# Two attentions, a latent part and a mixer's end reordered in a 2-block fp32 transformer kernel

## The reference

```
o = from_blocks(lax.map(block_fn, ...))            # A: softmax over picked keys, B: stick-breaking
return (o * jax.nn.silu(gate)) @ w_o
...
mod = cond @ w_mod + b_mod                         # cond = silu(c); six rows of 2048
h = _rmsnorm(x, pre_mix_g) * (1.0 + scale_a) + shift_a
proj = h @ w_in                                    # q_lat, kv_lat, k_rope, hq, f_fwd, f_bwd, hi, hg
attn_out = _mla(...)                               # rmsnorm(q_lat) @ w_uq, rmsnorm(kv_lat) @ w_ukv, rope, softmax
rec_out = _hgrn2_bidir(...)
mix = jnp.concatenate([attn_out, rec_out], axis=-1) @ w_out
x = x + gate_a * _rmsnorm(mix, post_mix_g)
h = _rmsnorm(x, pre_mlp_g) * (1.0 + scale_m) + shift_m
y = jnp.square(jax.nn.relu(h @ w_up)) @ w_down     # 2048 -> 8192 -> 2048
x = x + gate_m * _rmsnorm(y, post_mlp_g)
```

## Time and profile before

| | us |
|---|---|
| median of 3 runs | 2210.45 (2209.52 to 2211.97) |
| the profiled execution | 2210.13 |
| its span | 2208.3 |
| TensorE busy | 2170.7 |
| VectorE busy | 1429.2 |
| ScalarE busy | 1028.2 |

### The profile page before, as it was taken

How to read it: one execution, slowest core, us unless ns; L and a number is a source line. 1 busy time by engine, 2 the same in 40 slices (tenths; PEclk the granted TensorE clock), 3 DMA queues, 4 the chain that set the end, 5 groups by cost and what they waited for, 6 DMA issues and landing times.

```text
span 2208.3 us, 24626 instructions
## 1 busy us (share of the span) xinstructions
PE 2170.7 (98%) x10387; PEld 1808.1 (82%) x10387; DVE 1429.2 (65%) x1408; ACT 1028.2 (47%) x1044; POOL 7.2 (0%) x17
## 2 busy tenths in 40 slices
PE   8999999999999999999999999999999999999998
PEld 8878888877888788778788988877888888888887
DVE  5778667775756777877966676486445545544646
ACT  5443563433436643444454566575433433443442
POOL 0000000000000000000100000000000000000000
PEclk9999999999999999999999999999999999999999
DMA  8867649575976557758952325355556655655753
GB/s 289 311 243 271 248 153 364 205 292 183 366 270 231 189 223 296 274 193 355 346 178 98 129 86 200 115 229 215 204 193 230 225 191 210 248 191 191 267 182 123
DMA packets 73070, 497.25 MB, mean 225 GB/s; under 512 B 9040, under 2 KB 9472, under 8 KB 16384
## 3 DMA queue, kind: packets, MB, share of 16 engines
q1 hardware_dynamic: 72640, 495.59, 61.6%
q10 hardware_dynamic: 320, 0.09, 0.0%
HBM read 491.42 MB, written 4.23 MB: 224 GB/s over the span
## 4 chain that ended last, share of the span: by engine, by line
PE 91%; DVE 5%; ACT 2%; DMA 2%; issue 1%; DVEq 0%; SPq 0%; ACTq 0%
PE products L2395 65%; PE products L2406 14%; PE aside L2714 1%; DMA raw<-in_w_c_f 1%; PE transposed L2833 1%; DVE w_low L1470 1%; PE transposed L2471 1%; ACT w_high L851 1%; DVE raw L1484 1%; PE transposed L2561 1%; PE aside L2561 1%; PE transposed L2529 1%; DVE w_low_spare L1470 0%; PE products L2820 0%; PE aside L2820 0%
## 5 line engine op out<-in xcount | busy, mean ns | idle before, releaser
L1470 DVE TENSOR_TENSOR w_low<-raw,w_high 128x2048 fp32r<-128x2048 f32 (+3 forms) x323 | 714.4, 2215 | 551.6 <-ACT w_high L851 550.9
L851 ACT ACTIVATE w_high<-raw 128x2048 fp32r<-128x2048 f32 (+3 forms) x323 | 597.7, 1853 | 802.1 <-PE products L2395 635.9
L2395 PE MATMUL products<-w_high,x_high 128*128 128x512 f32 (+2 forms) x1664 | 641.7, 386 | 13.6 <-DVE w_low L1470 10.9
L2395 PE MATMUL products<-w_high,x_low 128*128 128x512 f32 (+2 forms) x1664 | 634.1, 381 | 0.0
L2395 PE MATMUL products<-w_low,x_high 128*128 128x512 f32 (+2 forms) x1664 | 633.9, 381 | 0.0
L2395 PEld LDWEIGHTS products<-w_high,x_high 128*128 128x128 f32 x1664 | 313.3, 188 | 73.7 <-issue 13.2
L2395 PEld LDWEIGHTS products<-w_high,x_low 128*128 128x128 f32 x1664 | 313.2, 188 | 59.2
L2395 PEld LDWEIGHTS products<-w_low,x_high 128*128 128x128 f32 x1664 | 313.3, 188 | 58.5 <-issue 1.7
L1484 DVE SCALAR_TENSOR_TENSOR raw<-raw,cond_row 128x2048 f32<-128x2048 f32 x96 | 220.3, 2295 | 0.8 <-DMA raw<-in_w_mod 0.8
L2395 PE MATMUL products<-w_high,u_high 128*128 128x512 f32 x496 | 193.7, 391 | 0.0
L2395 PE MATMUL products<-w_high,u_low 128*128 128x512 f32 x496 | 193.0, 389 | 0.0
(11 more groups left out here) (442 smaller groups left out, 2113.3 us busy)
## 6 DMA issues: line engine op xcount, KB each, us to landing
raw<-in_w_mlp SPq DMA_DIRECT2D x128, 1024.0 KB, 4.9
raw<-in_w_mod SPq DMA_DIRECT2D x96, 1024.0 KB, 5.1
raw<-in_w_ple SPq DMA_DIRECT2D x32, 1024.0 KB, 6.6
raw<-in_w_a_qkv SPq DMA_DIRECT2D x24, 1024.0 KB, 5.8
raw<-in_w_b_kvq SPq DMA_DIRECT2D x24, 1024.0 KB, 6.9
raw<-in_w_a_gate SPq DMA_DIRECT2D x16, 1024.0 KB, 6.1
raw<-in_w_a_out SPq DMA_DIRECT2D x16, 1024.0 KB, 7.2
raw<-in_w_b_gate SPq DMA_DIRECT2D x16, 1024.0 KB, 6.1
```

What stands on the lines that cost most here:

```text
L851: act.activation(split_tile(m, 0, st, u, j, 0, n), m.raw[:, RAW_SLOT[at], 0:n], ACT.Copy).then_inc(m.s_w_high, 1)
L1470: dve.tensor_tensor(lo, m.raw[:, RAW_SLOT[at], 0:n], hi.bitcast(F32), ALU.subtract).then_inc(m.s_raw_used, 1)
L2395: ins = pe.matmul(bank, x[:, x0 + kk, a], w, start=first and kk == 0 and n == 0, stop=last and kk == st.kq - 1 and n == 2)
```

## The change

Four places are written in another order. (a) Attention A: the four key heads of both row blocks are roped first, with half of the memset as the signal, the query heads behind. (b) Attention B: the last b_gate product is stored by a plain copy between the logarithms of groups 2 and 3, and its Silu is taken later, behind x_high of group 1; the gating of group 2 stands ahead of x_low of group 1. (c) Block C's latent part: two of three pieces of proj_mla are turned ahead of the last heads_slot; the last head's finish, low of ukv and c_oh, and ScalarE's copies of mla_kv are reordered. (d) The mixer's end: unit 0 of c_om is multiplied for row block 1 only up to j = 1; j = 2 and 3 of row block 1 stand behind all of row block 0. The mlp's units 0 and 1 are multiplied together: row block 0 with all eight quarters, then row block 1. All eight split quarters are kept in slots until then; one of the new spare slots is the memory of `cond_row`, so the cond row is loaded again behind them, its Silu taken in the mlp, and the mod tiles start two units later. The normed columns and thrown squares go into the PSUM banks `aside`.

```
-    ("c_om", 2, (0, 0), 4, 512), ("mlp", 32, (0, 2, 2, 0, 0, 0, 0, 0) * 4, 4, 512),
+    ("c_om", 2, (0, 0), 4, 512), ("mlp", 32, (0, 0, 0, 2, 2, 0, 0, 0) + (0, 2, 2, 0, 0, 0, 0, 0) * 3, 4, 512),
...
-SPARE_SLOTS = ((18432, 20480), (13312, 15360), (8192, 6144), (8192, 14336), (12288, 16384))
+SPARE_SLOTS = ((18432, 20480), (13312, 15360), (8192, 6144), (12288, 16384), (8192, 14336), (None, 22528), (10240, 4096))
...
-    m.h_cols = at("mlp_normed_columns", 22528, [P, 2, 512])
-    m.mix_sq = at("mix_squares", 23552, [P, 2, 512])
+    m.h_cols = m.u
...
-TURNS_MLP = {0: [(0, 2)], 1: [(0, 3)], 3: [(0, 4), (2, 5)], 4: [(0, 6)], 5: [(0, 7)]}
+TURNS_MLP = {(0, 0, 0): [(2, 3)], (1, 0, 2): [(3, 4)], (1, 0, 3): [(1, 5)], (0, 1, 0): [(1, 6)], (0, 1, 1): [(1, 7)]}
...
+    def cond_again():
+
+        sp.wait_ge(m.s_w_used, 4 * (PLAN["mlp"].g0 + 1) + 4 + 2)
+        bring(m.cond[:], rows(d.c, D), m.s_cond_landed)
...
-        load_unit("mlp", u, {(0, 1): x_rows})
+        load_unit("mlp", u, {(0, 0): x_rows, (2, 3): cond_again})
...
-    gemm("b_gate", keep(m.pb, 3072, ACT.Silu), late=2, aside=softplus_aside)
-    logs((2, 3))
+    def gate_kept(st, i, k):
+        if (i, k) == (1, 1):
+            logs([2])
+            keep(m.pb, 3072)(st, i, k)
+            logs([3])
+        else:
+            keep(m.pb, 3072, ACT.Silu)(st, i, k)
+
+    gemm("b_gate", gate_kept, late=2, aside=softplus_aside)
...
     group_high(1, m.s_b_ogt, m.s_b_xh)
+    act.wait_ge(m.s_g_free[1], (gate.s0 + gate.units) // 2 + 1)
+    last_gates = m.pb[:, :, 3072 + 1536:3072 + 2048]
+    act.activation(last_gates, last_gates, ACT.Silu).then_inc(m.s_b_gate3, 1)
...
+        if n == 6 * HH - 1:
+            latent_high(0)
+            latent_high(1)
         heads_slot(n)
...
-        if j < 3:
-            high_unit("c_oh", 0, [j])
-        if j == 1:
+        if j == 0:
             head_columns(14, 1)
+            high_unit("c_oh", 0, [0])
+        if j >= 2:
+            high_unit("c_oh", 0, [j - 1])
...
-    for rb in range(RB):
-        rope(m.pa[:, rb, 0:(NH + NKV) * HD].rearrange("p (h e) -> p h e", e=HD)[:, :, 0:2 * ROT_A], NH + NKV, ROT_A, 0, rb, m.a_rope)
-    dve.memset(m.a_nm[:], 0.0).then_inc(m.s_a_roped, 1)
+    for n, (first, heads) in enumerate(((NH, NKV), (0, NH))):
+        for rb in range(RB):
+            rope(m.pa[:, rb, HD * first:HD * (first + heads)].rearrange("p (h e) -> p h e", e=HD)[:, :, 0:2 * ROT_A], heads, ROT_A, 0, rb, m.a_rope)
+        dve.memset(m.a_nm[:, 2 * n:2 * n + 2], 0.0).then_inc(m.s_a_roped, 1)
...
     low_unit("b_out", 0, [2])
+    gate_group(2)
     group_low(1, m.s_b_xh, m.s_b_done)
-    gate_group(2)
...
-        for rb in range(RB):
-            ins = half(om, 0, j, m.g[:, 2 * k + rb], rb, 0, True, True)
+        for rb in range(RB if j < 2 else 1):
+            ins = half(om, 0, j, m.g[:, 2 * k + rb], rb, 0, True, j < 2)
...
+    for j in range(4):
+        pe.wait_ge(m.s_raw_used, quarter_at(om, 1, j) + 5)
+        half(om, 1, j, m.g[:, MIX_BANKS[0][j]], 0, 4, j < 2, True).then_inc(m.s_om_rows, 1)
+    for j in (2, 3):
+        pe.wait_ge(m.s_mix_added, j - 1)
+        half(om, 0, j, m.g[:, MIX_BANKS[1][j]], 1, 0, True, False).then_inc(m.s_w_used, 1)
+    early = {2: {0: lambda: turn(0), 2: lambda: turn(1)}, 3: {2: lambda: turn(2)}}
+    for j in range(4):
+        if j < 2:
+            pe.wait_ge(m.s_mix_added, 3 + j)
+        half(om, 1, j, m.g[:, MIX_BANKS[1][j]], 1, 4, j < 2, True, early.get(j)).then_inc(m.s_w_used, 1)
...
+    def first(st):
+        for rb in range(RB):
+            for u in range(2):
+                for c in range(4):
+                    between = {at: (lambda nth=nth: turn(nth)) for at, nth in TURNS_MLP.get((u, rb, c), ())}
+                    ins = half(st, u, c, m.g[:, 2 * u + rb], rb, 4 * c, c == 0, c == 3, between)
...
-    add_row(7, 0)
     mix_gain(0, 2)
+    first(0)
+    mix_gain(0, 3)
+    inverse_std(0, 1)
     dve.wait_ge(m.s_res2_landed, 16)
...
+    low_unit("mlp", 1, [1])
+    added(1, 3)
+    low_unit("mlp", 1, [2])
     second(1)
+    inverse_std(1, 2)
     scaled(1, 0)
+    low_unit("mlp", 1, [3])
```

More of the change, by code:

```diff
@@ L78 @@
 BY_ROWS = ("c_hi", "c_mla", "c_hg")
-PRODUCTS = {"uq": 4, "ukv": 4, "c_oh": 4, "c_om": 8}
+PRODUCTS = {"uq": 4, "ukv": 4, "c_oh": 4, "c_om": 6}
 LEAD = {0: (0, 0, 0, 0, 0), 2: (0, 0, 1, 1, 2), 3: (0, 0, 1, 2, 3)}
@@ L341, in memory @@
     m.hi, m.lo = sb("w_high", [P, RING, 2048], F32R), sb("w_low", [P, RING, 2048], F32R)
-    m.spare = [[at(f"w_{part}_spare_{n}", word, [P, 2048], F32R) for part, word in zip(("high", "low"), words)] for n, words in enumerate(SPARE_SLOTS)]
     m.xh, m.xl = sb("x_high", [P, KT, T], F32R), sb("x_low", [P, KT, T], F32R)
@@ L348, in memory @@
     m.cond = sb("cond_row", [P, D])
+    m.spare = [[nc.alloc_sbuf_tensor_at(f"w_{part}_spare_{n}", [P, 2048], F32R, offset=nc.lookup_mloc(m.cond).addr) if word is None
+                else at(f"w_{part}_spare_{n}", word, [P, 2048], F32R) for part, word in zip(("high", "low"), words)] for n, words in enumerate(SPARE_SLOTS)]
     m.modc = sb("mod_columns", [P, MOD_TILES])
@@ L552, in memory @@
     m.s_b_done = sem("b_done")
+    m.s_b_gate3 = sem("b_last_gate")
     m.s_m_ready = sem("m_ready")
@@ L1440, in quarter @@
                 mlp_high(q, 5, [1, 2])
-            elif k < 7 or not last:
+            elif (q, k) == (0, 0):
+                mlp_high(0, 2, range(3))
+            elif (q, k) != (0, 1) and (k < 7 or not last):
                 mlp_high(q, k + 1, range(3))
@@ L1448, in quarter @@
                 u_high(q, k - 1)
-            if k < 7 or not last:
+            if (q, k) > (0, 0) and (k < 7 or not last):
                 mlp_high(q, k + 1, [3])
+            if (q, k) == (0, 1):
+                act.wait_ge(m.s_cond_landed, 32)
+                act.activation(m.cond[:], m.cond[:], ACT.Silu).then_inc(m.s_cond_ready, 1)
     for q in range(4):
@@ L2153, in vector_program @@
         if rb == 0:
+            low(ukv, 0, [3])
             head_columns(14, 1)
@@ L2331, in hidden_quarter @@
                 low(mlp, 8 * q + 5, [1, 2])
-            elif k < 7 or not last:
+            elif (q, k) == (0, 0):
+                low(mlp, 2, range(3))
+            elif (q, k) != (0, 1) and (k < 7 or not last):
                 low(mlp, 8 * q + k + 1, range(3))
@@ L3058, in hidden_quarter @@
                 first(mlp)
+            elif first and k == 1:
+                pass
             elif k == 4:
```

219 lines of the change are left out of this document (123 added, 96 removed).

## The result

The changed kernel takes 2193.03 us (median of 4 runs, 2193.0 to 2195.17); the kernel before, timed beside it, 2210.12 (4 runs, 2209.52 to 2211.97). The ratio is 0.9924, with a 95% interval of 0.9909 to 0.9939: 17.1 us, 0.8%, faster. The forecast was 2193.8 (2191.0 to 2199.5). The profiled execution took 2193.03 too, its span is 2191.2 against 2208.3.

What follows compares the result with a forecast made beforehand. TensorE, busy 98% of the span, bounds the kernel, so only its waits and slow clock can go. 0.9 + 2.3 + 3.75 + 9.1 = 16.05, with 0.55 start-up 16.6 us off: about 2193.8 us, range 2191.0 to 2199.5.

Steps and rivals of the forecast that it cites:

- Attention A, 0.9: Attention A: roping key heads first makes keys ready near 215, removing TensorE's a_neg_max wait; 0.9 us, bounds 0 to 0.9.
- Attention B, 2.3: Attention B: earlier logarithms remove the 1.49 us b_scores wait, earlier group 2 gating b_out_gated's 0.82; bounds 1.5 to 2.5.
- Latent part, 3.75: Block C: waits for x_low (1.80), proj_hq (1.01) and mla_kv (1.04) go, less 0.1 new wait; bounds 2.0 to 4.0.
- Mixer's end, 9.1: Mixer's end into mlp: put-off quarters and joint units cover both row blocks' chains; gain 9.1 us, bounds 4.5 to 10.
- The late column of row block 0: Mixer's end: the last column of row block 0 was counted 0.4 us late, leaving that much wait.
- The first rival: Mixer's end: tight places with about half a us to spare are late, 3 to 5 us come back, 2197 to 2199; chance 0.20.
- the fourth: Rival: a new wait inside the mixer slows the clock again, losing 5 to 7 us, 2199 to 2201; chance 0.06.
- The slow clock: Behind the mixer's-end wait, TensorE's reduced clock cost 1.2 us in one stretch and some 0.6 in the next.
- The columns in PSUM, 0: Normed columns and thrown squares written to PSUM: the SBUF time of 1.49 us for four kept, no gain in the sum.
- Cond row, 0: Mlp: reloading the cond row and taking its Silu later costs 0, with 10 us to spare.
- The third rival: Loads queued behind the cond row's come late, making the whole slower, 2215 for 0.2%; chance 0.03.
- start-up: Slower first matmuls behind each removed wait, up to 0.2 us each; 0.55 us together for the earlier parts.

Runs made afterwards that it cites:

- all three undone: Changed kernel with attention A's key-heads-first rope, attention B's reordered logarithms and its early gating of group 2 all undone: 2197.94 us.
- the two runs show: Changed kernel with block C's whole latent part undone: 2196.46 us; with only its latent columns put behind the last heads_slot again: 2196.00 us.

## Why the prediction was right

**Attention A, 0.9.** Right, 1.12 with the slower matmuls behind the wait. In the timeline after, the keys' rope starts at 213.35 and the signal's memset stands at 215.23, where the prediction had about 215:

```profile
213.35 0.49 DVE L1604 TENSOR_TENSOR a_rope<-proj_a,cos_sin 128x128 f32<-128x128 f32 x2
...
215.23 0.07 DVE L1745 MEMSET a_neg_max<- 128x16 f32 x1
```

That it shows in the time is not shown by its own run (+0.2), only by the traces and by the run with all three undone.

**Attention B, 2.3.** Right, 2.72. ScalarE after, in the order of the earlier trace rows:

```profile
754.67 1.02 ACT L918 ACTIVATE proj_b<-products 128x1024 f32<-128x1024 f32 x1 [0.57 <-PE products L2450]
...
757.18 1.28 ACT L1139 ACT_TABLE_LOAD   x1
```

The product's copy now waits 0.57 us, for 2.16 in the earlier trace rows, and the table of Exp is loaded at 757.18 where the forecast said 757.6. The Silu put off ends at 781.7 and group 3's gating, at 784.05 on VectorE, waits for none of it. Undone singly, the logarithms cost 1.7; the gating brought its 0.82 us wait back and, by the rows, 1.0 to 1.1 us, but only 0.2 in the median.

**Latent part, 3.75.** Right, 3.91. The new wait is 0.3 us for mla_kv ahead of ukv's last product; 0.1 for w_low was expected. The wait for x_low goes for another reason than the other two, as the two runs show; those two were not undone singly.

**Mixer's end, 9.1.** Right, 9.57, and by its own steps. ScalarE, VectorE and TensorE there after:

```profile
1460.31 0.49 DVE L2295 TENSOR_SCALAR mix<-residual,rstd 128x512 f32<-128x512 f32 x1
...
1462.04 0.60 PE L3112 MATMUL transposed<-const,mix 128*128 128x128 f32 x4
...
1465.33 1.47 ACT L1402 ACTIVATE aside<-transposed,mlp_norm_columns 128x128 f32<-128x128 f32 x4
...
1485.61 0.49 DVE L2295 TENSOR_SCALAR mix<-residual,rstd 128x512 f32<-128x512 f32 x1
...
1488.30 0.60 PE L3112 MATMUL transposed<-const,mix 128*128 128x128 f32 x4
```

The first turn's rows are ready at 1460.8 and used at 1462.04: 1.2 us to spare, forecast 1.0. Row block 1's first rows are ready at 1486.1 and used at 1488.3: 2.2 to spare, forecast 1.9. The late column of row block 0 costs 0.19 us, forecast 0.4. Between c_oh and unit 2 the waits went from 7.1 us to 0.2 and TensorE's busy time fell by 2.6, where the forecast had 7.1 to 0.4 and 2.4 (1.8 of clock and 0.6 of small change). The first rival, that these slacks would go, didn't come, nor did the fourth, a new wait in the mixer; in the ten profiles that have the new order whole, the wait at that column is 0.49 at most. That TensorE's cover decides, and not the work moved, is shown by the two runs that change its order alone: they lose 3.44 and 7.29 us at the very turns where cover was taken away, 4.1 and 8 expected.

**The slow clock.** It was counted with 1.8 us, and TensorE's clock now reads 1.00 all through the mixer's end. By the granted clocks of the earlier trace rows it cost some 5 x 0.11 + 5 x 0.23 = 1.7 us, an estimate; the other 0.9 of the 2.6 us of busy time are then the slower matmuls behind the four waits. The Trainium skill (TensorE: Matmul & The Clock Gate, Part 1: The HAM clock gate) has an idle array fall back to the halved rate; the runs agree, the stretches with or behind waits of 3.44, 4.41 and 7.29 us read 0.77, 0.50 and 0.50.

**The columns in PSUM, 0.** Four scalings take 1.46 to 1.48 us after and took 1.49 to 1.51 before (the earlier trace rows has one). The tip of the Trainium skill (ScalarE: Activation LUTs, Step-by-step: what each stage is for), that PSUM is the faster destination for ScalarE, agrees in its direction; it is worth some 0.03 us per column here.

**Cond row, 0.** Right: 9.4 us to spare for the Silu. The third rival, the slower side, was about the loads behind the cond row's; the two waits for w_low in the list after stand at the start (8.9) and at c_f's end (1.46), none in the mlp, so those loads were not late either.

**What was mis-sized** is little. The earlier three parts gave 7.75 for 6.95, so 0.80 beyond their waits where 0.55 was allowed for start-up, and the mixer's end gave 0.47 more than its 9.1: 0.7 too little in all. The loss of 0.76 at the start and the gain of 0.58 at c_f's end, which nobody forecast, nearly cancel each other. So the profiled execution gained 17.1 us for 16.6 forecast; that it came so near is owed to mechanisms and sizes that were right, and in part to luck, since such events alone move other profiled runs by 2 to 5 us.

**What stays open.** Why the wait at c_f's end varies was not tried. Whether the 0.58 us there belong to the change can't be said: in eight profiles whose programs are the same up to that place it is between 0.88 and 2.80 us. Whether the loads there set its length is not shown either.

## What to carry to other kernels

Where one engine is the bound, write down for each of its waits the chain that ends it and the work that lies over it; if the chain is longer, put work of the bound engine in between that doesn't need its result, here two quarters and a second unit for row block 0, at the price of slots. Such steps added up here, part by part within 0.5 us, so they can be summed from a trace before anything is built. Judge a part of 1 us by landmarks in the traces, or undo several such parts at once: the spread of the medians hides one alone.
